# Differential attention: values held in TensorE, two query tiles side by side in each product, results turned back and scaled by ScalarE

## The reference, cut to what matters

```python
sc = einsum('bqhmd,bshmd->bhmqs', qb, k) * d ** -0.5        # two maps m, d = 64, s up to 2048
p  = softmax(where(mask, sc, NEG_INF), axis=-1)             # mask: key chunk <= query chunk
a  = p[:, :, 0] - lam * p[:, :, 1]
o  = einsum('bhqs,bshe->bqhe', a, v)                        # e = 128
o  = o * rsqrt(mean(o * o) + eps) * subln_g * (1 - lambda_init)
```

## Time and profile before

| what | value |
|---|---|
| three runs, median (lowest, highest) | 2617.49 us (2616.2, 2617.77) |
| profiled execution, its own time | 2614.33 us |
| its span | 2612.6 us |
| granted TensorE clock over the span | 0.973 |
| the phase of the change | TensorE from 518.3 to 1202.2 us, 683.9 us |
| TensorE busy over the span | 94% |
| VectorE, ScalarE busy over the span | 65%, 48% |

### The profile page before, as it was taken

One profiled execution on the slowest core, in us unless ns is written; L12 is line 12 of the kernel. 1 busy time (PEld: TensorE's weight loads), 2 busy tenths in 40 slices (PEclk: granted clock), 3 DMA queues, 4 the chain that ended last, 5 costly groups with the idle time before them and its releaser, 6 DMA issues. The chain is left out here.

```text
span 2612.6 us, 41848 instructions
## 1 busy us (share of the span) xinstructions
PE 2452.7 (94%) x12559; PEld 2058.7 (79%) x12560; DVE 1706.9 (65%) x3389; ACT 1258.7 (48%) x2177; POOL 439.7 (17%) x536
## 2 busy tenths in 40 slices
PE   6999999899999999998999998499999999999990
PEld 5888888778888888886888886488888888888880
DVE  6766666676776777776545544775775657657856
ACT  4444333444544545444111112575775657757856
POOL 1111111110111101100233331121111111111110
PEclk9999999999999999999999999699999999999995
DMA  6333443576656657445544433687898779768957
GB/s 226 105 105 106 131 128 105 144 201 193 209 184 199 202 179 228 160 152 209 171 144 123 134 137 129 265 298 240 313 346 257 254 245 352 256 228 313 389 147 265
DMA packets 229964, 533.75 MB, mean 204 GB/s; under 512 B 25985, under 2 KB 92801, under 8 KB 227825
## 3 DMA queue, kind: packets, MB, share of 16 engines
q1 hardware_dynamic: 160880, 420.18, 46.4%
q0 software_dynamic: 16416, 56.57, 8.9%
q10 hardware_dynamic: 52576, 55.87, 6.1%
HBM read 413.53 MB, written 119.01 MB: 204 GB/s over the span
## 5 line engine op out<-in xcount | busy, mean ns | idle before, releaser
L2693 DVE TENSOR_TENSOR e_wl<-rw_raw,e_wh 128x1024 fp32r<-128x1024 f32 (+1 forms) x384 | 446.6, 1219 | 26.1 <-ACT e_wh L2606 25.9
L2606 ACT ACTIVATE e_wh<-rw_raw 128x1024 fp32r<-128x1024 f32 (+1 forms) x384 | 377.1, 1050 | 4.0 <-PEq L74 4.0
L2556 PE MATMUL e_p_gu<-e_wh,e_xh 128*128 128x512 f32 (+1 forms) x784 | 310.6, 396 | 0.8 <-DVE e_xl L2698 0.8
L2558 PE MATMUL e_p_gu<-e_wl,e_xh 128*128 128x512 f32 (+1 forms) x784 | 306.2, 391 | 0.0
L2557 PE MATMUL e_p_gu<-e_wh,e_xl 128*128 128x512 f32 (+1 forms) x784 | 305.7, 390 | 0.0
L1379 ACT ACTIVATE b_th<-b_t 128x512 fp32r<-128x512 f32 (+3 forms) x160 | 85.3, 533 | 261.4 <-PE b_t L1298 253.2
L1486 DVE TENSOR_SCALAR_CACHE_REDUCE b_sc<-b_s 128x512 f32<-128x512 f32 (+4 forms) x320 | 175.8, 580 | 36.8 <-PE b_s L1287 34.6
L414 PE MATMUL j_pg<-qkv_w_hi,jb_xh 128*128 128x512 f32 (+1 forms) x512 | 191.8, 375 | 6.6 <-DVE qkv_w_lo L750 6.6
L416 PE MATMUL j_pg<-qkv_w_lo,jb_xh 128*128 128x512 f32 (+1 forms) x512 | 187.6, 366 | 0.0
L415 PE MATMUL j_pg<-qkv_w_hi,jb_xl 128*128 128x512 f32 (+1 forms) x512 | 186.8, 365 | 0.0
L1320 PE MATMUL b_pg<-jb_w_low,jb_xh 128*128 128x512 f32 x512 | 179.6, 405 | 1.3 <-DVE b_g_out L1546 0.9
(11 more groups left out here) (428 smaller groups left out, 6002.6 us busy)
## 6 DMA issues: line engine op xcount, KB each, us to landing
rw_raw<-w_gate_up SPq DMA_DIRECT2D x256, 512.0 KB, 7.6
rw_raw<-w_down SPq DMA_DIRECT2D x128, 512.0 KB, 9.2
jb_xh<-xt_hi SPq DMA_DIRECT2D x62, 512.0 KB, 3.7
jb_xl<-xt_lo SPq DMA_DIRECT2D x62, 512.0 KB, 4.9
gates<-b_g_out ACTq DMA_DIRECT2D x64, 256.0 KB, 5.5
m_gt<-gates SPq DMA_DIRECT2D x16, 1024.0 KB, 9.3
jb_lead<-qk_hi SPq DMA_DIRECT2D x36, 256.0 KB, 6.4
jb_lead<-qk_lo SPq DMA_DIRECT2D x36, 256.0 KB, 7.7
```

The costliest lines, as they stand in the source:

```text
L2556: nc.tensor.matmul(p_gu[p][:], xh[:, at], hi, start=(k == 0), stop=False)
L2558: last = nc.tensor.matmul(p_gu[p][:], xh[:, at], lo, start=False, stop=(k == KD - 1))
L2606: nc.scalar.activation(wh[:, slot(e, s), :], raw[:, s:s + 1, :], ACT.Copy).then_inc(w_hi, 1)
L2693: nc.vector.tensor_tensor(wl[:, slot(e, s), :], raw[:, s:s + 1, :], f(wh[:, slot(e, s), :]), ALU.subtract).then_inc(w_lo, 1)
```

## The change

The step becomes a **pair** `p` of query tiles (2p and 2p+1) and a group `j` of 256 keys: 36 steps for each head. The values are now the stationary operand, and the transposed weights of both tiles move through it side by side: for each 128 keys one product of 512 columns (high values with high and low weights of both tiles) and one of 256 (low values with high weights). The result comes out transposed, so after a pair's last step ScalarE copies one half of it (`leave_part`), VectorE adds the other (`sum_parts`), TensorE turns both tiles back (`turn_back`), and ScalarE scales them into `o` (`finish`). GpSimd's addition is gone; a pair is stored in one DMA.

The two transpose banks now serve `turn` and `turn_back` in the order of `events`. The score buffers still hold four tiles, which are two pairs. The scores of a pair are made during the pair before it, its exponentials too, and `ratios` (inverse and coefficient for both tiles) and the first `combine` stand at the last step of the pair before. The lists for scores, exponentials, combines and gates are written anew. A head still has 384 gate products. In heads 1 to 3 they lie, first half and second half of a step: 16 and 8 in step 0, 17 and 7 in step 1, 24 and 0 in step 2, 3 and 11 in step 6, 4 and 4 in step 26, 4 and 0 in step 27. A pair's scores and exponentials have these steps: pair 1 all in step 0, pair 2 in steps 1 and 2, pair 3 in steps 3 to 5, and so on; the last step before a pair is 0, 2, 5, 9, 14, 20, 27, and 35 for the next head.

```diff
-    AHEAD = 3
+    RING = 4
+    PAIRS = NQ // 2
+    PAIR_KEYS = 2 * P
-    steps = [(i, g) for i in range(NQ) for g in range(groups[i])]
+    steps = [(p, j) for p in range(PAIRS) for j in range(p + 1)]
...
+        ratios_at[end].append((more, q))
+        combine_at[end].append((more, q, 0))
...
+    LATENCY = {0: 5.0, 1: 2.0, 2: 3.0, 5: 1.5, 9: 1.0}
...
-            def values_of(h, i, g):
...
-                for c in range(ks.start, ks.stop, P):
-                    b, bs = c // P, slice(c - ks.start, c - ks.start + P)
-                    vb = vhl[g][:, b % 4]
-
-                    if b:
-                        nc.tensor.matmul(po[:, 0:BV], tl[:, n % 2, bs], vb[:, 0, :], start=False, stop=False)
-                    last = nc.tensor.matmul(po[:], th[:, n % 2, bs], vb.rearrange("p s d -> p (s d)"), start=(b == 0), stop=(0 < b == i))
-                    if not b:
-                        last = nc.tensor.matmul(po[:, 0:BV], tl[:, n % 2, bs], vb[:, 0, :], start=False, stop=(b == i))
...
+            def values_of(h, p, j):
...
+                for c in range(2):
+                    b = 2 * j + c
+                    v_high, v_low = (vhl[b // 4][:, b % 4, s, :] for s in range(2))
+                    qs_of = slice(P if b == 2 * p + 1 else 0, PAIR_KEYS)
+                    nc.tensor.matmul(po[:, :, qs_of], v_high, thl[:, n % 2, c, :, qs_of], start=(b == 0), stop=False)
+                    last = nc.tensor.matmul(po[:, 0, qs_of], v_low, thl[:, n % 2, c, 0, qs_of], start=False, stop=(b == 2 * p + 1))
...
+            def turn_back(k):
+
+                pe.wait_ge(o_summed, k + 1)
+                bank_free(back_event[k])
+                for a in range(2):
+                    last = nc.tensor.transpose(pt[back_event[k] % 2][:, a * P:(a + 1) * P], o_turned[:, a * P:(a + 1) * P], ident[:])
+                last.then_inc(o_back, 1)
...
             for h in range(B_HEADS):
-                for n, (i, g) in enumerate(steps):
-                    for more, j, c in scores_at[n]:
+                for n in range(GB):
+                    for more, i, c in scores_at[n][0]:
                         if h + more < B_HEADS:
-                            scores_of(h + more, j, c)
+                            scores_of(h + more, i, c)
                     gate(h, n, 0)
+                    if steps[n][1] == 0 and pair_at(h, n):
+                        turn_back(pair_at(h, n) - 1)
                     if n + 1 < GB:
                         turn(h, *steps[n + 1])
                     elif h + 1 < B_HEADS:
                         turn(h + 1, *steps[0])
+                    for more, i, c in scores_at[n][1]:
+                        if h + more < B_HEADS:
+                            scores_of(h + more, i, c)
                     gate(h, n, 1)
-                    values_of(h, i, g)
+                    values_of(h, *steps[n])
+            turn_back(PAIRS * B_HEADS - 1)
...
+            def leave_part(k):
+                h, p = divmod(k, PAIRS)
+                act.wait_ge(pv, GB * h + first[p + 1])
+                nc.scalar.activation(part_hi[:], po[:, 0, :], ACT.Copy).then_inc(part_left, 1)
+
+            def finish(k):
+                act.wait_ge(o_back, k + 1)
...
+                for a in range(2):
+                    last = nc.scalar.activation(o[:, k % 2, a, :], pt[back_event[k] % 2][:, a * P:(a + 1) * P], ACT.Copy,
+                                                scale=inv[:, (2 * k + a) % (2 * RING), 0:1])
...
+            def sum_parts(k):
+                dve.wait_ge(part_left, k + 1)
...
+                nc.vector.tensor_tensor(o_turned[:], po[:, 1, :], part_hi[:], ALU.add).then_inc(o_summed, 1)
...
-                    nc.gpsimd.tensor_tensor(o[:, i % 2, :], parts[:, i % 2, 0, :], parts[:, i % 2, 1, :], ALU.add).then_inc(added, 1)
+                    pool.dma_start(ob_pair(p, h), o[:, k % 2]).then_inc(stored[k % 2], 16)
```

More of the change, by code:

```diff
@@ L1042, in gates_from, with width_of @@
[L1042 to L1052 removed]
+    def width_of(i, j):
+        return min(PAIR_KEYS, (i + 1) * P - j * PAIR_KEYS)
@@ new lines, in diff_attention_phase @@
+    for p in range(PAIRS):
+        for j in range(1, p + 1):
+            combine_at[max(first[p] + j - 2, first[p] - 1)].append((0, p, j))
+    events, turn_event, back_event = [("turn", 0)], {0: 0}, {}
+    for m in range(GB * B_HEADS):
+        if steps[m % GB][1] == 0 and m:
+            back_event[len(back_event)] = len(events)
+            events.append(("back", len(back_event) - 1))
+        if m + 1 < GB * B_HEADS:
+            turn_event[m + 1] = len(events)
+            events.append(("turn", m + 1))
@@ new lines, in diff_attention_phase, with pair_at, blocks_at, span @@
+    back_event[len(back_event)] = len(events)
+    events.append(("back", len(back_event) - 1))
+    def pair_at(h, n):
+        return PAIRS * h + steps[n][0]
+    PASSES = 3 * KD
+    def blocks_at(n):
+        return scores_at[n][0] + scores_at[n][1]
+    def span(made):
+        return sum(keys(i, g).stop - keys(i, g).start for _, i, g in made) / P
+    LATENCY = {0: 5.0, 1: 2.0, 2: 3.0, 5: 1.5, 9: 1.0}
+    vec = [1.1 + 0.5 * len(combine_at[n]) + 0.4 * (len(combine_at[n]) > 0) + 0.3 * len(blocks_at(n)) + 0.27 * span(blocks_at(n)) + 0.5 * (steps[n][1] == 0)
+           for n in range(GB)]
@@ new lines, in diff_attention_phase, with gates_from @@
+    sca = [0.7 + 1.1 * (steps[n][1] == 0) + sum(0.25 + 0.11 * (i + 1) for _, i, _ in exps_at[n]) for n in range(GB)]
+    ten = [1.15 + 0.228 * span(blocks_at(n)) + 0.12 * len(blocks_at(n)) for n in range(GB)]
+    def gates_from(start, done_before=0):
+        fill = [max(max(vec[n], sca[n], 1.5) * 1.3 - ten[n], 0.3) + LATENCY.get(n, 0.0) if n >= start else 0.0 for n in range(GB)]
+        places = [(n, half) for n in range(start, GB) for half in range(1 if 0 < steps[n][0] == steps[n][1] else 2)]
+        share = [fill[n] / sum(1 for at in places if at[0] == n) for n, _ in places]
+        order = [(u, q) for u in range(done_before, NT) for q in range(PASSES)]
+        parts, made = {}, 0
+        for at, place in enumerate(places):
+            due = len(order) if place == places[-1] else round(len(order) * sum(share[:at + 1]) / sum(share))
+            parts[place] = order[made:max(due, made)]
+            whole = [n for n, (_, q) in enumerate(parts[place]) if q == PASSES - 1]
+            if whole and place != places[-1] and (place[1] or len(parts[place]) - whole[-1] < PASSES // 2):
+                parts[place] = parts[place][:whole[-1] + 1]
+            made += len(parts[place])
@@ L1526, in low @@
[L1526 to L1532 removed]
+                for a in range(2):
+                    i, w = 2 * p + a, width_of(2 * p + a, j)
+                    u, ks = i % RING, slice(j * PAIR_KEYS, j * PAIR_KEYS + w)
+                    last = nc.vector.scalar_tensor_tensor(at[:, n % 2, a, 0:w], sc[u][:, 1, ks], coef[:, u:u + 1], sc[u][:, 0, ks], ALU.mult, ALU.add)
@@ L1550, in low_lead, with made @@
                 nc.vector.tensor_tensor(lead[:, LEAD + s, :], chunk0.rows[:, s % 2, :], f(lead[:, s, :]), ALU.subtract).then_inc(lead_lo, 1)
-            for i in range(AHEAD):
-                if i == 2:
-                    lambda_of_sums()
-                    invert(0, 0)
-                    weigh(0, 0)
-                    combine(0, 0, 0)
-                for g in range(groups[i]):
-                    copies(0, i, g)
-                maximum(0, i)
-                bias(0, i)
-                if i == 0:
-                    lambda_sums()
-            ready = []
+            def made(h, blocks):
+                for more, i, c in blocks:
+                    if h + more < B_HEADS:
+                        copies(h + more, i, c)
+                        if c == groups[i] - 1:
+                            maximum(h + more, i)
+                            bias(h + more, i)
+            made(0, [(0, 0, 0)])
+            lambda_sums()
+            made(0, [(0, 1, 0)])
+            low_w(0, 4)
+            lambda_of_sums()
+            low_w(0, 5)
+            ratios(0, 0)
+            combine(0, 0, 0)
             for h in range(B_HEADS):
-                for n, (i, g) in enumerate(steps):
-                    begun = [(h + more, j) for more, j, c in combine_in(h, n) if c == 0 and h + more < B_HEADS]
-                    low(h, i, g)
+                for n, (p, j) in enumerate(steps):
+                    low(h, n)
                     for u in ended_in[h][n - 1][1] if n else ():
```

337 lines of the change are left out of this document (156 added, 181 removed).

## The result

The median of four runs is 2712.0 us (2705.1 to 2717.3) against 2616.8 us (2615.0 to 2617.8): a ratio of 1.0363, 95% interval 1.0338 to 1.0388. The direction was forecast; the size was not: 95 us more where 46 were expected, and 21 us above the upper end of the range. The profiled execution took 2713.8 us (span 2712.1).

What follows compares the result with a forecast made beforehand. TensorE's own work was taken as the bound. Products -16.8, head starts +10.9, clock +4.5, head 0 +8.8, gate bank +17.4, pair ends +19.6 and phase end +1.7 made +46.1 us: 2664 us, range 2626 to 2691.

Steps and rivals of the forecast that it cites:

- Products: TensorE's value products and transposes over the phase: 181 us before, 164 us after, 16.8 us less.
- 35 gives 1.3: Pair-end wait of TensorE's turn for the combine in step 35, a head's last: 1.3 us, gate weights in front.
- The head's start: Second turn of heads 1 to 3 waits 5.0 us for a longer chain, 1.3 before: 10.9 us more.
- Gate bank: TensorE's next gate tile waits for VectorE's gate bias: 5.0 us a head, 2.9 in head 0, 17.4 in all.
- Pair ends: Turns at pairs' last steps wait for exponentials, ratios and combines: 26.1 us, three quarters taken, 19.6 us.
- The walk: Step-by-step sums of VectorE's and TensorE's work; gate bank: step 6 waits 1.6, step 31 1.5, six others 3.8 together.
- Head 0: First head: waits and clock falls add 15.5 us, against old waits and one clock fall that go: 8.8 us more.
- the third rival: The clock falls to half behind short waits too, 16 x 1.7 = 27 us more: 2691 us, chance 9%.
- lost to the clock: Half clock behind the longer head-start waits, 1.5 us each: 4.5 us in three heads, besides head 0's share.

Runs made afterwards that it cites:

- e8: e3 with each product of the low value part done twice, 31.9 us more TensorE work: 2695.2 us.
- e1: The changed kernel with the last two k and v pieces of the next head loaded inside that head, only SyncE's list changed: 2680.1 us.
- e3: The changed kernel with e1's spread loads and, in a head's last step, gate weight 4's low half behind VectorE's ratios, combines and gate bias: 2677.1 us.
- e14: The kernel before the change with its k and v loads bunched at the head's end like the changed kernel's, only SyncE's list changed: 2647.9 us.
- e5: e3 with the scores of the next head's tiles 2 and 3, and tile 2's exponentials, made in steps 34 and 35 instead of step 0: 2672.5 us.
- e13: e3 with the last four pairs' scores ended a step earlier and the planner told of more latency, which moves gate products into waiting steps: 2691.4 us.
- e4: The changed kernel with 45 turns of the identity ahead of the waiting first turn in heads 1 to 3: 2708.9 us.
- e17: The changed kernel with only the last two k pieces of the next head loaded inside that head, v loads as they were: 2681.3 us.

## Why the forecast had the direction right and fell 49 us short

- **Products: right.** The groups of the kernel after by shape count 144 + 112 products of 512 and as many of 256 columns, with no idle time before them; in the kernel after's timeline below they start 0.24 and 0.11 us apart, against 0.23 and 0.12.

```profile
719.96 0.40 PE L1378 MATMUL b_po<-b_thl,b_v 128*128 128x512 f32 x1
...
720.20 0.27 PE L1379 MATMUL b_po<-b_thl,b_v 128*128 128x256 f32 x1
...
720.31 0.40 PE L1378 MATMUL b_po<-b_thl,b_v 128*128 128x512 f32 x1
```

The 1088 "narrow" products before were half of them 256 columns wide; what a pair of them costs, 0.23 us, is what the sum used. It may look as if the saving was credited too high, since TensorE's work is worth only 0.57 of itself in e8. But the forecast worked out its waits against the new, shorter products, so they hold already what the saving adds to them. The table below has the term as measured.

- **The step that failed:** "35 gives 1.3 (three of the moved gate weights are in front)". The wait was seen, at the right place and behind the right instructions, but the weights were counted as if their data were there: 0.62 us each. Nobody followed their loads. ScalarE waited 6 to 8 us for the DMA, and VectorE's list stood behind it; TensorE stood for 7.4, 9.3 and 8.6 us and not 1.3. With the wait for `jb_xl` (5.4 us) and the half clock behind them this is **32 us** by e1, 35 by e3, and e14 brings the like about without the change. SyncE's lists of the two kernels showed it: `load_k` at 26 to 29 of 36 steps where it was at 25, 29, 33 of 40 and in the next head.

- **The head's start:** right. The second turn waited 3.0, 2.8 and 3.8 us in the kernel after, where TensorE came to it at half clock, and 4.6 us in e1 and e3, where it did not; 5.0 was forecast. The two rows of e1's timeline on either side of it:

```profile
723.35 0.38 PE L1340 MATMUL b_t<-ident,b_o_turned 128*128 128x128 f32 x2
728.18 1.12 PE L1332 MATMUL b_t<-ident,b_at 128*128 128x128 f32 x4 [4.45 <-DVE b_at L1574]
```

- **Gate bank: a third too small. Pair ends: good.** At the gate bank e3 has 33 waits, 26.4 us by the profile and 31 to 32 us counted from the products' distance, against 17.4 and head 0's 4.3 forecast. The walk had eight places in a head with 6.9 us, of which it took the small ones at half, 5.0 us, since they "may vanish". They did not: head 1 of e3 has eight waits, 5.5 us by the profile, 6.7 by distance. Head 0 has ten, 11.0 us, where 7.2 were forecast. The turns' waits of e3, 36.8 us, less the second turns (three of 4.45 and head 0's 7.1) leave 16.3 us, 19 by distance, against 19.6 for the ends of pairs. That these waits can't be taken away singly was not said; e5 to e13 show it.

- **Head 0:** its second turn waited 7.5 us (5.6 forecast) and the gate bank in step 2 4.2 (4.3). With its loads in order it still takes 198.7 us in e3 against 179.6: 19 us more, of which 1.6 are a later start, where 8.8 and head 0's shares of the other terms (2.9 and 3.7, less 4.2 of products) made 11.

- **The clock:** the third rival, half clock behind short waits, was partly true. Behind the waits of 4.6 us it fell each time. Behind short ones both are seen. In the kernel after there is a fall behind the 2.04 us wait that ends at 659.31, and none behind the 1.48 us wait that ends at 888.98. In e1 the twin of the second wait, again 1.48 us (it ends at 875.40), has the fall that this one lacks, so the length of the single gap does not decide it (windows of the kernel after, then of e1, clock third from the end):

```profile
661.20:664.20 3.00, 3.00 (x12) 2.60 (x11) 1.40 (x4) 0.98 (x2) 0.00 (x0) 0.50 0.18 64
885.00:895.00 10.00, 8.21 (x44) 6.60 (x43) 6.22 (x15) 5.08 (x9) 0.72 (x1) 1.00 1.04 226
```

```profile
877.00:880.00 3.00, 3.00 (x7) 2.33 (x8) 1.53 (x4) 0.52 (x1) 0.00 (x0) 0.50 1.08 221
```

The Trainium skill, "TensorE: Matmul & The Clock Gate" (section "A second HAM failure mode: psum-queue depth-cycling"), says that frequent short idle times between groups of matmuls make the clock swing. The trace agrees in part: here it swings behind some of the short gaps and not behind others.

- **The sum against the phase as measured.** Cut into windows of 0.5 us, the phase divides into TensorE's waits, what the granted clock took of its busy time (busy time times one less the clock), and the rest, its work at full clock: 9.4, 4.0 and 670.5 us before, 91.7, 25.7 and 659.3 in the kernel after, 68.3, 12.3 and 660.5 in e3. The table has what each kernel has above the kernel before, in us. In it 8 us (some 50 waits more at 0.16 us each) are moved from work to waits, to count as the forecast does, so its first and third rows are estimates to 2 us or so. Of the forecast's head 0, 7.5 us are waits and 1.3 clock.

| in the phase | forecast | kernel after | e3 |
|---|---|---|---|
| TensorE's waits | +57.1 | +90 | +67 |
| lost to the clock | +5.8 | +22 | +8 |
| TensorE's work at full clock | -16.8 | -19 | -18 |
| together | +46.1 | +92.7 | +57.2 |

The work term came out as forecast. Of the 33 us of waits that the forecast lacks in the kernel after, the head ends are 22, `jb_xl` 8 and the gate bank 9, while the second turns, reached later, wait 5 us less than forecast. Of the clock's 22 us, e3 gives 13 back by removing the long waits; e4 gave back 5 by keeping TensorE busy in them, and little of that showed. e3's 10 us of waits above the forecast are the gate bank's. Outside of the phase the profiled execution is 7 us longer than that of the kernel before (1.6 ahead of it, 5 behind it), e3's 3 us; that was not followed.

No version that computes the same beats the kernel before: the best, e5, is at 2672.5 us. A likely reason, argued and not tried: the new form wants a whole pair's exponentials before its first turn, where before a tile's were made ahead of need.

## What to carry to other kernels

When a change renumbers steps, walk the DMA queue's list as carefully as the engines': for each load ask what is queued ahead of it and which engine's in-order list will stand on it. A wait forecast behind an instruction has two parts, that instruction's duration and its own operands' arrival. Do not halve small waits in the hope that they vanish: here nearly all of them stayed. And a saving on one engine counts in full only beside waits that were worked out with the shorter work; what a us on either engine is worth by itself is measured by adding work to each (here about 0.57 and 0.4).

## What was not expected of the hardware

- 2 MB of k loads taken out of the last ten steps of each head are worth 31 us (e17), without a change to any other engine's list. At the head's end of the kernel after, the issue of a single load held SyncE for 4 to 5 us, where it takes 0.3 to 0.5 at other times. The rows of the kernel after (the v load has 256 KB, the x load 512 KB), and then the v load's in e1:

```profile
706.22 5.05 SPq L1179 DMA_DIRECT2D jb_w<-v_lo  x1
711.33 4.06 SPq L1191 DMA_DIRECT2D jb_xh<-xt_hi  x1
715.43 0.43 SPq L1192 DMA_DIRECT2D jb_xl<-xt_lo  x1
```

```profile
717.60 0.50 SPq L1179 DMA_DIRECT2D b_v<-v_lo  x1
```

The program has no wait of its own between a piece's `v_hi` and `v_lo` load. So the queue, as these rows read, pushes back on the engine that feeds it, and everything behind in its list is late by that, beside its own longer landing.
